# Four row norms of the retention ahead of the next units' states, one rotation behind two scores, first logits a half job later

## The chip, the cores and the metric

The kernel runs on one core of a Trainium2 chip. The metric is the device time of one execution in microseconds (us), the lower the better. Matrix products are done by TensorE (PE in the profile), most other arithmetic by VectorE (DVE), ScalarE (ACT) and GpSimd (POOL); SyncE (SP) issues most transfers. Each engine works through its own instructions in program order and waits on semaphores for the others.

## What is computed

One step of a one-layer streaming encoder on 512 prompt tokens, 64 sample tokens and 16 meta tokens, width 1024:

```
h = rmsnorm(x) @ w_in                        # rq, rk, rv, rg, sq, sk, sv
o_r = retention(rope(rq), rope(rk), rv)      # 4 heads, a state per head, chunk by chunk
o_r = rmsnorm(o_r) * silu(rg)                # per head: "row norm"
o_s = sliding_window_attention(sq, sk, sv)   # 8 query heads, 2 key heads, window 128
x = x + concat(o_r, o_s) @ w_out
x = x + moe(rmsnorm(x))                      # 32 experts, top group, then 2 in it
```

The experts' gate, up and down weights are 32 x 3 matrices of 1 MB; the router's logits come from the new x.

## The kernel before

The tokens are five tiles in the order `ORDER = [4, 0, 1, 2, 3]`; tile 4 (TAIL) holds the 64 sample and 16 meta tokens, the others 128 prompt tokens each. A *job* is the product of one tile with one 512-column chunk of w_in or w_out over half of the 1024 rows (12 matmuls, `job`, L1098; 8 for the tail, L1092). Jobs are numbered in the order of `halves()`: 10 for each of the chunks SKV, SQ, RQK, RV, RG and OUT0, OUT1 (the two halves of w_out). Weights are split into a high and a low part: ScalarE writes `w_hi` (L1648), GpSimd `w_lo` (L901).

All small work of retention, attention and router is hung between the jobs by `plan()`: for each job number s there are three lists, `before[s]`, `after[s]` and `behind[s]`, and the order of the whole program is before[s], job s, after[s], behind[s], for s = 0, 1, 2 and so on. **Every engine walks through this one list** and emits its own share of each step, so moving a step moves it on every engine that has a share in it. A step that only VectorE has a share in moves on VectorE alone.

The retention has ten units m = 0..9 (`RUNITS`: each tile twice, for the even and the odd heads). r0 is job 40, the first RG job. The steps of a unit:

- `ra` (two units at a time): TensorE the score products (L1230), VectorE the causal mask `ret_aT` (L2060).
- `ro` (two units at a time on TensorE): state increments (L1203), outputs of scores (L1257) and of the state (L1263). ScalarE squares the output (L1731). VectorE `ret_out`: two operations update the state (L2073, L2074, semaphore st_new), two form the mean square (L2076, L2079, semaphore ms_ready). GpSimd `ret_root`: eleven small operations (L316 to L326), then root_ready.
- `rn`, on VectorE alone (`ret_norm`): output times gate into `h_a` (L2107; waits for the gate), then times the root into `o_rows` (L2111; waits for root_ready).
- `rm`: TensorE transposes `o_rows` (L1291), VectorE multiplies by the gain (`part_r`, L2121), ScalarE writes the high part (L1737), VectorE the low part (L2126).

In the program order before, `rn` of units 1, 3 and 5 stands behind the `ro` of units (2, 3), (4, 5) and (6, 7), and `rn` of unit 6 behind the `ro` of (8, 9). The gate of a tile comes from its RG job (`gate_of`, L2090). `post(RQK, t)` is the rotary embedding of a tile's retention queries and keys (`rope`, L1911 to L1913, then L1971 and L1972), on VectorE; its first reader is the transpose `rT` (tile 0: job 39). The attention has 20 units; `score` (VectorE: row maxima, L2017 to L2025; ScalarE: exponentials), `norm` (VectorE, L2031 to L2034), `pT` (TensorE transposes of `probs`, L1170 and L1172), `value`.

After an OUT job VectorE adds it to x (`evict`, L2143). `square` is ScalarE's, `hT` transposes the new x on TensorE (L1302) and scales it on VectorE (L2155), `logit` multiplies by the router's weights on TensorE (L1313) and copies the result on VectorE (L2162, L2166). Behind the last logits come the choice of experts (VectorE), the gathering of rows and 16 pairs of experts (L1370 gate and up, L1385 down). SyncE loads their weights into a ring of 18 buffers of 1 MB; a load waits until TensorE has read what lay in its buffer:

```
sp.wait_ge(gu_ps, p - 2)
load_gu(p)
```

The first loads of experts' weights wait for all ten units' `rm`.

Of the kernel before, what the change touches and what calls it, by code (L numbers as in the profile page):

```python
# [21 lines left out]
TAIL = 4  # L22
# [32 lines left out]
SKV, SQ, RQK, RV, RG = range(5)  # L55
# [4 lines left out]
ORDER = [TAIL, 0, 1, 2, 3]  # L60
# [34 lines left out]
def plan():  # L95
# [3 lines left out]
    before = [[] for _ in range(len(lots) + 8)]  # L99
    after = [[] for _ in range(len(lots) + 8)]  # L100
    behind = [[] for _ in range(len(lots) + 8)]

    def done(c, t):
        return at[c, t, 1]
# [20 lines left out]
    for c in range(2, OUT0 + 2):  # L125
        first = at[c - 1, ORDER[0], 0]
        for k in range(KD):
            s = first + (k + 1 if k < 4 else 8 + (k - 4) // 2)
# [5 lines left out]
    s = done(SKV, ORDER[-1])  # L134
# [9 lines left out]
    for t in ORDER:  # L144
        s = done(SQ, t)
# [10 lines left out]
        before[s + 1 + n % 2].append(("norm", n))  # L156
        after[s + 3 + n % 2].append(("value", n))
    for t in ORDER:
        before[done(RQK, t) + 1].append(("post", RQK, t))
    before[30] += [("counts",)]  # L160
    for n, s in enumerate(starts):
        after[s + 2 + n % 2].append(("pT", n))
# [4 lines left out]
    r0 = at[RG, ORDER[0], 0]  # L167
# [4 lines left out]
        after[done(RG, t)].append(("gate", t))  # L172
    behind[done(RG, TAIL)].append(("gate2", TAIL))
    late = [3, 4, 5, 6, 7, 8, 11, 12, 13, 14]
    for m, (t, par) in enumerate(RUNITS):

        after[r0 + m // 2 * 2].append(("ra", m))
        (after if m > 1 else behind)[r0 + m // 2 * 2 + 1].append(("ro", m))
        before[r0 + late[m] - (1 if m > 5 else 0)].append(("rn", m))
    for m in reversed(range(len(RUNITS))):  # L180
        after[r0 + late[m]].insert(len(after[r0 + late[m]]) if m in (1, 3, 5, 6, 7) else 0, ("rm", m))
    after[r0 + len(RUNITS) + 1].append(("states_out",))
# [2 lines left out]
    for n in range(2):  # L185
        for i, t in enumerate(ORDER):
            s = done(OUT0 + n, t)
            after[s].append(("square", n, t))
            after[s + 1].append(("hT", n, t))
            after[s + 2].append(("logit", n, t))  # L190

    last = at[OUT1, ORDER[-1], 0]
    after[last - 1].append(("choose",))
# [136 lines left out]
def stream_step(nc, consts, x_prompt, x_sample, cache_ret_state, cache_swa_k, cache_swa_v,  # L330
# [21 lines left out]
    with ExitStack() as ctx:  # L352
# [334 lines left out]
        kv_out = sem("kv_out")  # L687

        STEPS = plan()

        def evicted(j):
# [1864 lines left out]
```

## Time and profile before

| | before |
|---|---|
| device time, median of 3 runs | 555.42 us (555.2 to 555.72) |
| the profiled execution: its own time, its span | 555.36 us, 553.5 us |
| PE, PE weight load busy | 483.5 us (87%), 304.8 us (55%) |
| DVE, ACT, POOL busy | 271.9 us (49%), 132.6 us (24%), 155.2 us (28%) |
| moved by DMA, mean | 144.74 MB, 262 GB/s |

The span runs from the first to the last instruction; the 1.86 us between it and the execution's own time lie around it. The shares are means over stages with different limits, so the rows below are read by stage. All row times are us from the start of the span. "[0.82 <-DVE o_rows L2111]" at the end of a row says how long the engine had stood idle just before, and which instruction ended that.

### The profile page before, as it was taken

Reading aid. Unit: us, or ns where it says so; the run is one execution under the profiler, and the core shown is the slowest. Engines: PE = TensorE matmul, PEld = TensorE weight load, DVE = VectorE, ACT = ScalarE, POOL = GpSimd, SP = SyncE. Lnnn points to the kernel's source line nnn. Section 1 sums busy time; section 2 is a strip of 40 time slices with the busy share of each in tenths; the row PEclk is TensorE's granted clock in tenths of the full one; section 3 lists DMA queues with packets and bytes.
Section 4 is the critical chain, followed back from the end, with each engine's and each line's share of the span. In section 5 each row is a group of like instructions: output and inputs, shape, how many; then the busy total and the mean of one; then the engine's idle time right before and its main releaser. Section 6 shows DMA issues by size and latency. Waiting matters only on the chain.

```text
span 553.5 us, 7556 instructions
## 1 busy us (share of the span) xinstructions
PE 483.5 (87%) x2748; PEld 304.8 (55%) x2748; DVE 271.9 (49%) x619; ACT 132.6 (24%) x361; POOL 155.2 (28%) x280
## 2 busy tenths in 40 slices
PE   4976989899999999899993999889999868878884
PEld 4955867677776677678883743233433323233232
DVE  2869679888455575742267422313332222022535
ACT  4754355465455223222111100000000000000010
POOL 5445773042024455823003300111112111000003
PEclk9989999899998999999996899979999999889998
DMA  8440220130039603249969699999999999999996
GB/s 299 161 126 7 76 77 2 35 119 1 2 124 319 234 8 102 83 178 401 388 249 422 234 342 420 408 420 417 424 416 418 419 423 418 418 422 420 414 399 216
DMA packets 35031, 144.74 MB, mean 262 GB/s; under 512 B 5842, under 2 KB 8994, under 8 KB 23216
## 3 DMA queue, kind: packets, MB, share of 16 engines
q1 hardware_dynamic: 26320, 129.94, 60.0%
q0 software_dynamic: 4528, 9.01, 4.5%
q10 hardware_dynamic: 4144, 5.28, 2.9%
q8 instruction: 23, 0.38, 0.3%
q14 instruction: 16, 0.13, 0.1%
HBM read 138.16 MB, written 17.30 MB: 281 GB/s over the span
## 4 chain that ended last, share of the span: by engine, by line
PE 44%; DVE 16%; DMA 14%; SPq 11%; issue 5%; ACT 5%; POOL 1%; DVEq 0%; ACTq 0%; POOLq 0%
PE banks L1098 15%; PE banks L1370 10%; SPq L743 7%; DMA w_moe_b<-in_w_up_dram 5%; PE banks L1385 4%; SPq L751 3%; DMA w_moe_b<-y_d 3%; DMA y_d<-rows,idx 2%; PE banks L1364 2%; DMA rows<-hn_d,idx 1%; DMA y_d<-y_sb,idx 1%; ACT w_hi L1648 1%; PE banks L1460 1%; PE banks L1313 1%; PE banks L1160 1%
## 5 line engine op out<-in xcount | busy, mean ns | idle before, releaser
L901 POOL TENSOR_TENSOR w_lo<-w_raw,w_hi 128x512 fp32r<-128x512 f32 x52 | 70.2, 1365 | 112.1 <-ACT w_hi L1648 110.6
L1370 PE MATMUL banks<-w_moe_b,xgT 128*64 128x512 f32 x224 | 66.9, 618 | 10.6 <-DMA w_moe_b<-in_w_up_dram 6.8
L1370 PE MATMUL banks<-w_moe_a,xgT 128*64 128x512 f32 x224 | 67.7, 626 | 4.2 <-DMA w_moe_a<-in_w_up_dram 4.2
L2376 DVE SCALAR_TENSOR_TENSOR glu_b<-banks,wr,glu_a 128x256 f32<-128x256 f32 x15 | 7.2, 483 | 96.5 <-ACT glu_a L1780 96.5
L1780 ACT ACTIVATE glu_a<-banks,wr 128x256 f32<-128x256 f32 x15 | 7.1, 473 | 196.2 <-PE banks L1370 183.3
L1098 PE MATMUL banks<-w_hi,xT_hi_a 128*128 128x512 f32 (+3 forms) x124 | 51.1, 412 | 1.5 <-DVE xT_lo_a L1842 1.5
L1098 PE MATMUL banks<-w_lo,xT_hi_a 128*128 128x512 f32 (+3 forms) x124 | 48.7, 393 | 0.0
L1098 PE MATMUL banks<-w_hi,xT_lo_a 128*128 128x512 f32 (+3 forms) x124 | 48.5, 391 | 0.0
L1370 PEld LDWEIGHTS banks<-w_moe_b,xgT 128*64 128x64 f32 x224 | 20.9, 142 | 49.4 <-issue 46.6
L1098 PE MATMUL banks<-w_hi,xT_hi_b 128*128 128x512 f32 (+3 forms) x92 | 35.6, 387 | 0.8 <-issue 0.8
L1370 PEld LDWEIGHTS banks<-w_moe_a,xgT 128*64 128x64 f32 x224 | 21.4, 144 | 26.0 <-issue 24.3
L1098 PE MATMUL banks<-w_lo,xT_hi_b 128*128 128x512 f32 (+3 forms) x92 | 34.1, 370 | 0.0
L1098 PE MATMUL banks<-w_hi,xT_lo_b 128*128 128x512 f32 (+3 forms) x92 | 33.9, 369 | 0.0
L1648 ACT CAST w_hi<-w_raw 128x512 fp32r<-128x512 f32 x52 | 30.8, 614 | 12.5 <-DMA w_raw<-in_w_out_dram 11.1
L1385 PE MATMUL banks<-w_moe_a,actT 128*64 128x512 f32 x144 | 32.6, 593 | 0.5 <-DVE actT L2393 0.5
L1098 PEld LDWEIGHTS banks<-w_hi,xT_hi_a 128*128 128x128 f32 (+1 forms) x124 | 24.2, 195 | 7.0 <-ACT xT_hi_b L1590 1.7
L1701 ACT ACTIVATE probs<-banks,soft,rstd_hq 128x208 f32<-128x208 f32 x36 | 18.6, 519 | 35.2 <-DVE soft L2025 35.2
L1098 PEld LDWEIGHTS banks<-w_hi,xT_lo_a 128*128 128x128 f32 (+1 forms) x124 | 24.1, 195 | 5.1
L1098 PEld LDWEIGHTS banks<-w_lo,xT_hi_a 128*128 128x128 f32 (+1 forms) x124 | 24.3, 196 | 3.9
L951 POOL DMA_INDIRECT rows<-hn_d,idx x7 | 7.2, 1032 | 58.4 <-DMA y_d<-rows,idx 47.6
L2339 DVE TENSOR_TENSOR xgT<-banks,g_both 128x1024 f32<-128x1024 f32 x15 | 18.3, 1217 | 10.6 <-PE banks L1364 10.6
L1385 PEld LDWEIGHTS banks<-w_moe_a,actT 128*64 128x64 f32 x144 | 11.0, 137 | 19.9 <-issue 19.2
(361 smaller groups left out, 910.1 us busy)
## 6 DMA issues: line engine op xcount, KB each, us to landing
w_moe_a<-in_w_down_dram SPq DMA_DIRECT2D x20, 1024.0 KB, 20.4
w_moe_a<-in_w_gate_dram SPq DMA_DIRECT2D x16, 1024.0 KB, 12.1
w_moe_a<-in_w_up_dram SPq DMA_DIRECT2D x16, 1024.0 KB, 14.3
w_moe_b<-in_w_gate_dram SPq DMA_DIRECT2D x14, 1024.0 KB, 17.0
w_moe_b<-in_w_up_dram SPq DMA_DIRECT2D x14, 1024.0 KB, 17.3
w_moe_b<-in_w_down_dram SPq DMA_DIRECT2D x10, 1024.0 KB, 25.8
w_raw<-in_w_in_dram SPq DMA_DIRECT2D x34, 256.0 KB, 4.1
y_d<-in_consts_dram SPq DMA_DIRECT2D x9, 512.0 KB, 10.0
```

Source lines behind the costliest of these rows:

```text
L743: sp.dma_start(units(gu_at(p, e, m), 1)[:, 0, :], v[2 * p + e]).then_inc(gu_in[p % 4], 16)
L751: sp.dma_start(dn_at(p, e), down_v[2 * p + e]).then_inc(dn_in[p % 4], 16)
L901: nc.gpsimd.tensor_tensor(w_lo[:, s, :], w_raw[:, s, :], w_hi[:, s, :].bitcast(F32), ALU.subtract).then_inc(split, 1)
L951: pool.indirect_dma_start(out=xg(p), out_offset=None, in_=hn_d, in_offset=bass.IndirectOffsetOnAxis(ap=idx[:, p:p + 1], axis=0), bounds_ch ...
L1098: l = mm(into[0:R, 0:width], a, w, start=(kk == 0 and q == 0), stop=(kk == KD - 1 and q == 2))
L1364: l = nc.tensor.transpose(into[:, k // 4, (k % 4) * P:(k % 4) * P + P], gv[:, k, :], ident)
L1370: l = mm(acc[64 * e:64 * e + 64, u, :].rearrange("p (m f) -> p m f", m=2), xgT[:, xu, k, 64 * e:64 * e + 64], units(at_e[e], 2)[:, :, k * ...
L1385: l = mm(acc[64 * e:64 * e + 64, 2 + n, :], actT[:, j, 64 * e:64 * e + 64], mats[e][:, j * D + n * 512:j * D + n * 512 + 512], start=(j == ...
L1648: nc.scalar.copy(w_hi[:, s, :], w_raw[:, s, :]).then_inc(hi_done, 1)
L1701: af(probs[:, q, c2, :], sideA[:, b, 256 * c2:256 * c2 + KEYS], ACT.Exp, scale=rstd_hq[:, t, c2, u:u + 1], bias=soft[:, q, 2 + c2:3 + c2], ...
L2339: tt(xgT[:, u], at[:, 0:2, :].rearrange("p b (j n) -> p (b j) n", j=4), g2T.unsqueeze(2).to_broadcast([P, KD, P]), ALU.mult).then_inc(xg_e ...
L2376: stt(out=glu_b[:, :], in0=acc[:, u, 0:FF], scalar=scales[0], in1=glu_a[:, :], op0=ALU.mult, op1=ALU.mult).then_inc(done, 1)
```

## The change

Three edits to `plan()`; no instruction is added, removed or changed in shape.

```diff
     for t in ORDER:
-        before[done(RQK, t) + 1].append(("post", RQK, t))
+        (behind if t == ORDER[1] else before)[done(RQK, t) + 1].append(("post", RQK, t))
...
     late = [3, 4, 5, 6, 7, 8, 11, 12, 13, 14]
+    sooner = {2: 1, 4: 3, 6: 5, 8: 6}
     for m, (t, par) in enumerate(RUNITS):
 
         after[r0 + m // 2 * 2].append(("ra", m))
+        if m in sooner:
+            after[r0 + m // 2 * 2 + 1].append(("rn", sooner[m]))
         (after if m > 1 else behind)[r0 + m // 2 * 2 + 1].append(("ro", m))
-        before[r0 + late[m] - (1 if m > 5 else 0)].append(("rn", m))
+        if m not in sooner.values():
+            before[r0 + late[m] - (1 if m > 5 else 0)].append(("rn", m))
...
-            after[s + 2].append(("logit", n, t))
+            after[s + (3 if n == 0 and t == TAIL else 2)].append(("logit", n, t))
```

What it does to the list of steps:

- `rn` of unit 1 goes from before job 44 to behind job 43, ahead of `ro` 2 and 3; `rn` 3 from before 46 to behind 45, ahead of `ro` 4 and 5; `rn` 5 from before 48 to behind 47, ahead of `ro` 6 and 7; `rn` 6 from before 50 to behind 49, ahead of `ro` 8 and 9. All of these lie behind the gate or `rm` step of the same job.
- `post(RQK, 0)` goes from before job 24 to behind it: on VectorE it then follows `value` 4 and `score` 6 and 7, and still precedes `norm` 6, which is the first step before job 25.
- `logit` of the first half of the tail goes from behind job 53 to behind job 54, after `rm` 9 and just ahead of `hT` of tile 0.

## Rows read from the trace of the kernel before

**Rows 1.** Windows: busy us (count) of PE, PEld, DVE, ACT, POOL; granted clock; DMA share; GB/s

```profile
183.00:290.00 107.00, 101.11 (x559) 79.67 (x559) 56.10 (x140) 24.40 (x57) 39.86 (x106) 1.00 0.54 203
294.70:308.10 13.40, 6.59 (x24) 5.76 (x24) 9.48 (x43) 1.76 (x4) 2.23 (x8) 0.50 0.87 362
...
329.00:520.00 191.00, 168.40 (x792) 66.93 (x791) 54.37 (x83) 7.24 (x15) 25.31 (x25) 0.96 1.01 415
```

**Rows 2.** Waits, 180 to 240 us: who waited for whom, us in total, times, longest

```profile
PE banks L1291 <- DVE o_rows L2111: 4.3, 4, 1.8
```

**Rows 3.** Timeline of TensorE: start, us, line, count, idle before

```profile
193.97 0.33 PE L1291 MATMUL banks<-cst,o_rows 64*128 64x64 f32 x2 [0.82 <-DVE o_rows L2111]
...
205.11 0.44 PE L1291 MATMUL banks<-cst,o_rows 128*128 128x128 f32 x2 [0.83 <-DVE o_rows L2111]
...
216.16 0.44 PE L1291 MATMUL banks<-cst,o_rows 128*128 128x128 f32 x2 [0.84 <-DVE o_rows L2111]
...
225.80 0.50 PE L1092 MATMUL banks<-w_hi,xT_hi_a 128*128 128x512 f32 x1 [0.30 <-POOL w_lo L901]
...
228.31 0.44 PE L1291 MATMUL banks<-cst,o_rows 128*128 128x128 f32 x2 [1.77 <-DVE o_rows L2111]
...
236.53 0.63 PE L1313 MATMUL banks<-w_router,xgT 128*64 128x36 f32 x8 [1.21 <-DVE xgT L2155]
```

**Rows 4.** Timeline of VectorE in the retention

```profile
190.04 0.42 DVE L2073 TENSOR_TENSOR h_b<-banks,state_p 64x256 f32<-64x256 f32 x1 [1.27 <-ACT squares L1731]
...
193.04 0.42 DVE L2107 TENSOR_TENSOR h_a<-banks,gate 64x256 f32<-64x256 f32 x1
193.49 0.42 DVE L2111 TENSOR_TENSOR o_rows<-h_a,root_r 64x256 f32<-64x256 f32 x1
...
198.44 1.53 DVE L2126 TENSOR_TENSOR xT_lo_a<-part_r,xT_hi_a 128x256 fp32r<-128x256 f32 x1 [0.47 <-ACT xT_hi_a L1737]
...
201.17 0.42 DVE L2073 TENSOR_TENSOR h_b<-banks,state_p 64x256 f32<-64x256 f32 x1 [0.55 <-ACT squares L1731]
...
212.22 0.42 DVE L2073 TENSOR_TENSOR h_b<-banks,state_p 64x256 f32<-64x256 f32 x1 [2.31 <-ACT squares L1731]
...
222.61 0.42 DVE L2073 TENSOR_TENSOR h_b<-banks,state_p 64x256 f32<-64x256 f32 x1 [1.72 <-ACT squares L1731]
```

**Rows 5.** Timeline of GpSimd: ends of roots, start of a pair of roots, the splits behind it

```profile
183.27 0.19 POOL L326 TENSOR_TENSOR root_r<-root_r 64x2 f32<-64x2 f32 x1
...
198.04 0.19 POOL L326 TENSOR_TENSOR root_r<-root_r 128x2 f32<-128x2 f32 x1
198.41 1.27 POOL L901 TENSOR_TENSOR w_lo<-w_raw,w_hi 128x512 fp32r<-128x512 f32 x1 [0.18 <-POOL root_r L326]
...
209.30 0.20 POOL L326 TENSOR_TENSOR root_r<-root_r 128x2 f32<-128x2 f32 x1
213.71 0.19 POOL L316 TENSOR_SCALAR root_r<-ms_r 128x2 int32<-128x2 int32 x1 [4.21 <-DVE ms_r L2079]
...
220.56 5.19 POOL L901 TENSOR_TENSOR w_lo<-w_raw,w_hi 128x512 fp32r<-128x512 f32 x4 [0.18 <-POOL root_r L326]
```

**Rows 6.** Timeline of ScalarE behind the last states

```profile
231.91 0.94 ACTq L1745 DMA_DIRECT2D out_dram<-state_p  x2
...
234.09 0.40 ACT L1737 CAST xT_hi_a<-part_r 128x256 fp32r<-128x256 f32 x1
```

**Rows 7.** Timeline of VectorE and TensorE around `norm` 6

```profile
101.01 0.59 DVE L2034 TENSOR_TENSOR probs<-probs,soft 128x416 f32<-128x416 f32 x1
...
101.66 0.44 PE L1170 MATMUL banks<-cst,probs 128*128 128x128 f32 x2 [2.25 <-DVE probs L2034]
```

**Rows 8.** The chain that ended last: two jobs of twelve matmuls

```profile
103.55 4.46 PE banks L1098 x12
...
109.09 2.79 PE banks L1098 x12
```

**Rows 9.** Timeline of SyncE's queue

```profile
329.13 0.33 SPq L743 DMA_DIRECT2D w_moe_a<-in_w_gate_dram  x1
```

## Prediction, made before the changed kernel was run

> **What bounds the kernel now.** I read the windows first [rows 1]. From 183 to 290 us TensorE is busy for 101.1 of 107 us at full clock while the DMA engines have a share of 0.54: the projections and the retention are bound by TensorE, so an idle microsecond of TensorE there is a microsecond of the kernel. From 329 to 520 the DMA share is 1.01 at 415 GB/s: the experts are bound by the stream of weights. What matters is whether a gain before 290 gets through that stream. The first load of the saturated stretch is issued at 329.13 [rows 9], and by the code it waits for `gu_ps`, a product of TensorE, since its buffer must first be read. All earlier loads wait in the same way for work that follows the projections. So the stream starts when TensorE lets it, has a fixed length, and ends earlier by what TensorE gains. I count the gain in full.
>
> Next, who holds TensorE up. The table of waits from 180 to 240 has 4.3 us in four waits of the transposes of `rm` for `o_rows` [rows 2]. The timeline places them: 0.82 at 193.97, 0.83 at 205.11, 0.84 at 216.16 and 1.77 at 228.31, before `rm` of units 1, 3, 5 and 6. Two more are small: 0.30 at 225.80 for a `w_lo` of GpSimd, 1.21 at 236.53 before the first logits [rows 3].
>
> **The four norms.** A norm is two operations of 0.42 us, 0.87 from 193.04 to 193.91 [rows 4]. In the case of unit 1, VectorE did the states of 2 and 3 from 190.04, then the norm, and TensorE began its transpose at 193.97, 0.06 after the norm ended. Moved ahead of the states, a norm is ready some 3 us earlier, and the stall is gone if nothing else is late. What must hold:
>
> - *VectorE has a gap in front of the states.* It stood idle for 1.27, 0.55, 2.31 and 1.72 us before the four first state operations, always for ScalarE's squares [rows 4]. A norm of 0.87 fits into three of the gaps and delays the states of 4 and 5 by 0.3 us. Those states are read by TensorE only with the next tile, about 10 us later, so 0.3 costs nothing. Without the gaps each norm would put 0.87 on the states and on the masks behind them.
> - *The root is there.* An early `rn` that waits for `root_ready` holds `ro` behind it on VectorE, and through ms_ready also GpSimd. The roots of units 1 and 3 ended at 183.46 and 198.23, before VectorE is at the moved norm (188.8 and about 199.1). That of 5 ended at 209.50 [rows 5]. VectorE gets to it when `rm` 4 is done: 209.9 in the old timetable, 208.25 once 0.82 + 0.83 are saved. The root itself moves only by 0.5 (its mean square follows the states of 4 and 5, now started at 200.7 instead of 201.17), to 209.0. The norm's second operation then waits 0.3 and ends at 209.5, still ahead of the squares, which move from 212.22 to 210.57. The root of 6 belongs to the pair begun at 213.71, both over before the split at 220.56; the moved norm starts at about 218.4. All four fit, the third by about 1 us.
> - *GpSimd's splits.* Here a part is lost. Behind the roots of 6 and 7 GpSimd has four splits, 5.19 us from 220.56, ending 225.75; TensorE already waited 0.30 for the last at 225.80 [rows 3, 5]. The start of this run hangs on the mean square of unit 6 at 213.71, which comes from TensorE's outputs of tile 2. They lie ahead of the third stall, so they move by 0.82 + 0.83 = 1.65, not by 2.49. The last split ends at 224.1; TensorE, 2.49 earlier, would want it at 223.0. It waits 1.1 instead of 0.3: the third stall's 0.84 goes into a longer wait for `w_lo`.
> - The fourth, 1.77, is saved in full: `rn` 6 ends near 219.3, and `rm` 6 is wanted at 224.9. What is late next is `rn` 7, still behind the states of 8 and 9: with these at 220.1 and 4.7 us long as before, it ends at 225.8, against 227.9 when `rm` 7 is wanted.
>
> **The first logits.** Before, `hT` of the tail was held up on VectorE behind the low part of `rm` 7, and that behind ScalarE: it issued the states' transfers up to 232.85, did its square, and wrote the high part of `rm` 7 at 234.09 [rows 6]. With TensorE 3.4 us ahead, the whole chain moves by 3.4, since ScalarE is released by VectorE's `part_r` of unit 6, which follows the `evict` of job 51; the transposed tail is ready at about 231.9. At its old place TensorE would want it at 231.75 and stall for 0.2 (1.3 if a GpSimd split holds VectorE there). At the new place, after job 54 and `rm` 9, it is wanted at 234.8: no stall. That takes 1.21. On VectorE the clear of the logits and the copy (0.4 us together) move behind `rm` 9 and ahead of the scaling of tile 0's transpose, wanted only a job later. The new neighbour to watch is `hT` of tile 0 on TensorE, which needs `evict` of job 53: ready at 234.5, wanted at 235.4. No transfer is moved past any queue by these edits; the early experts' loads start some 5 us sooner, with the end of `rm` 9, ahead of the second half of w_out's weights as before.
>
> **The rotation.** It goes behind `value` 4 and the scores 6 and 7, but stays ahead of `norm` 6. TensorE stood idle for 2.25 us before 101.66 for exactly this norm, which ran from 101.01 [rows 7]; VectorE has the same operations to do ahead of it in either order, so the norm ends when it did. ScalarE gets its exponentials 3 us sooner and VectorE saves a wait after the norm, but no TensorE wait follows there until the stage ends. Its reader, `rT`, is 15 jobs away. I take 0. The bounds: were the stall to vanish, 2.25, and with it the slow stretch behind it, where a job took 4.46 us against 2.79 at full clock [rows 8]: 3.9 together. If the order costs, then by one contended operation of about 1.1 us.
>
> **Sum.** 0.82 + 0.83 + 0.84 + 1.77 + 1.21 = 5.47, less 0.84 for the splits: 4.6. The profiled execution took 555.36, the median is 555.42, so 0.06 apart; 555.42 - 4.6 gives **550.8 us**. One term I can't place: TensorE ran at granted clock 0.50 from 294.7 to 308.1 [rows 1], after the logits. If the return to full clock does not move with the work, up to 1.7 us more or less of it are slow, which is up to 0.9 either way; I take 0.
>
> **The rivals.**
>
> - *VectorE gives much of it back by contention* (0.13). One `L2126` took 1.53 us instead of 0.42, started at 198.44 just behind a split of GpSimd at 198.41 and ending 0.3 after it [rows 4, 5]. The moved norms of 3 and 6 come right beside splits, at about 199.5 and 218.9 to 224.1, and the last writes of `rm` 7 and 8 may too. Two or three hits of 1.1 in a row between 218 and 234 add 2.2 to 3.3; 0.9 of it is slack before tile 0's `hT`. Gain 2.2 to 3.3, 552.1 to 553.2. The Trainium skill (SBUF — State Buffer, "Who interferes with whom") says that a VectorE operation with two SBUF inputs and a GpSimd operation reading SBUF exclude each other, so that the second blocks fully; by that rule this rival is what moving a norm beside a split does, and the trace of this case agrees with its 1.53 us.
> - *GpSimd's splits keep up* (0.08): the four splits finish sooner (fewer neighbours) and the 0.84 is kept, with the 0.30: 549.7 to 550.0.
> - *The rotation frees `norm` 6 after all* (0.05): 3.9 more, 546.9.
> - *No change* (0.06): the stream of weights takes up the gain, because a load before 329 hangs on bytes and not on TensorE. Against it: [rows 9]. 555.4.
> - *Slower* (0.03): the early norms wait for roots, with states, masks and GpSimd's next roots queued behind them. It decides the sign when a root comes later than the squares by more than the stall it removes, about 1.4 + 1.2 us after the time I gave for unit 5. With two chains of roots late (3.3 us each, 6.6 for the pair before 220.4) each of four norms costs up to 1.9 beyond its slack, 7.6 against 5.5 gained: 557.5. Against it are the times of the roots in [rows 5].
>
> **How the numbers follow.** My forecast, the sum with its GpSimd term, has 0.65: 550.8, of its own 549.7 to 551.9, by the clock term of 0.9 and 0.2 for rounding. The contended case adds 0.13 above it, the kept splits 0.08 below, the rest lies outside. The range 549.4 to 553.2 takes in these three less their edges, about 0.8. Within 0.2% (1.1 us) of 555.42 is what a measurement of this kernel can't tell from no change. Faster: 0.65 + 0.13 + 0.08 + 0.05 = 0.91; the same 0.06; slower 0.03.
>
> **What would show it.** In the profile after, the waits of L1291 for `o_rows` are gone or below 0.2 us in sum; the wait of L1092 for `w_lo` at about 224 has grown from 0.30 to about 1.1; the wait of L1313 at the first logits is gone; `rm` 9's transposes come about 5 us earlier than before, the first saturated load at about 324.5 instead of 329.13, and the 2.25 us before `norm` 6's transposes are unchanged. I am wrong if a new wait for `o_rows`, `ret_aT` or `x_sb` stands in the retention, if `root_ready` holds VectorE for over 1 us, or if TensorE's clock falls in a further stretch between 183 and 290 us: each job in it costs 1.7.

## The result, and the profile after

| | before | after |
|---|---|---|
| device time, median | 555.57 us (555.2 to 556.88) | 550.43 us (546.18 to 551.61) |
| ratio after to before, 95% interval | | 0.9859 (0.9823 to 0.9894) |
| the profiled execution: its own time, its span | 555.36 us, 553.5 us | 550.74 us, 548.9 us |

The kernel became faster. The comparison puts the gain at 7.8 us (5.9 to 9.8, by the ratio of 555.57), which is 547.6 us against 555.42: more than I forecast, and below the low end of my range, 549.4. The plain median of the four executions, 550.43, lies near the forecast; they reach from 546.18 to 551.61, wider than my whole allowance for the clock. So there are two questions: did the predicted waits go, and were they of the size I gave them?

Lines of the changed kernel stand 4 higher (L1291 is now L1295, L901 is L905). The table of waits of the kernel after, 175 to 240 us (who waited for whom: us in total, times, longest), answers to [rows 2]. TensorE's wait of the transposes for `o_rows` has no row any more. What is left for TensorE is `w_lo`:

```profile
PE banks L1096 <- POOL w_lo L905: 0.8, 2, 0.5
```

TensorE's timeline of the kernel after, against [rows 3]: start, duration, line, shapes, count, idle before.

```profile
193.18 0.72 PE L1234 MATMUL banks<-rT 64*128 64x128 f32 x8
193.73 0.28 PE L1295 MATMUL banks<-cst,o_rows 64*128 64x64 f32 x2
...
203.92 0.44 PE L1295 MATMUL banks<-cst,o_rows 128*128 128x128 f32 x2
...
214.06 0.44 PE L1295 MATMUL banks<-cst,o_rows 128*128 128x128 f32 x2
...
223.29 0.50 PE L1096 MATMUL banks<-w_hi,xT_hi_a 128*128 128x512 f32 x1 [0.34 <-POOL w_lo L905]
...
224.53 0.50 PE L1096 MATMUL banks<-w_hi,xT_hi_a 128*128 128x512 f32 x1 [0.50 <-POOL w_lo L905]
224.87 0.39 PE L1096 MATMUL banks<-w_lo,xT_hi_a 128*128 128x512 f32 x1
225.09 0.38 PE L1295 MATMUL banks<-cst,o_rows 128*128 128x128 f32 x2
...
234.68 0.38 PE L1295 MATMUL banks<-cst,o_rows 128*128 128x128 f32 x2
234.99 0.66 PE L1317 MATMUL banks<-w_router,xgT 128*64 128x36 f32 x8
```

All four stalls before `rm` of units 1, 3, 5 and 6 are gone, and so is the one before the first logits (the last row stands without a bracket). The wait for `w_lo` has grown from 0.30 to 0.84, in two pieces.

VectorE and GpSimd of the kernel after, against [rows 4, 5]; first VectorE:

```profile
190.79 0.42 DVE L2077 TENSOR_TENSOR h_b<-banks,state_p 64x256 f32<-64x256 f32 x1 [0.49 <-ACT squares L1735]
...
199.97 0.98 DVE L2115 TENSOR_TENSOR o_rows<-h_a,root_r 128x256 f32<-128x256 f32 x1
...
208.64 0.42 DVE L2111 TENSOR_TENSOR h_a<-banks,gate 128x256 f32<-128x256 f32 x1
...
209.49 0.43 DVE L2115 TENSOR_TENSOR o_rows<-h_a,root_r 128x256 f32<-128x256 f32 x1 [0.44 <-DVE h_a L2111]
...
211.02 0.42 DVE L2077 TENSOR_TENSOR h_b<-banks,state_p 64x256 f32<-64x256 f32 x1 [1.11 <-ACT squares L1735]
...
219.20 1.45 DVE L2115 TENSOR_TENSOR o_rows<-h_a,root_r 128x256 f32<-128x256 f32 x1
```

```profile
199.39 1.27 POOL L905 TENSOR_TENSOR w_lo<-w_raw,w_hi 128x512 fp32r<-128x512 f32 x1 [0.18 <-POOL root_r L330]
...
209.16 0.20 POOL L330 TENSOR_TENSOR root_r<-root_r 128x2 f32<-128x2 f32 x1
...
212.51 0.19 POOL L320 TENSOR_SCALAR root_r<-ms_r 128x2 int32<-128x2 int32 x1 [3.16 <-DVE ms_r L2083]
...
219.10 5.37 POOL L905 TENSOR_TENSOR w_lo<-w_raw,w_hi 128x512 fp32r<-128x512 f32 x4 [0.18 <-POOL root_r L330]
```

Times of two traces are compared best from a common point: `rm` 0 stands at 185.89 before and at 186.64 after, so what comes after it is another 0.75 us earlier, counted from there, than the printed times say. The norms sit in VectorE's gaps: before the states of 4 and 5, and of 8 and 9, no idle time is left, before those of 6 and 7 1.11 us. The root of unit 5 ended at 209.36, and `rn` 5 went on at 209.49, 0.44 late by the row (forecast 0.3); the row names `h_a`, which was done at 209.06, so it is the root that it waited for. GpSimd's four splits begin at 219.10, 1.46 earlier by the printed times and 2.21 earlier behind `rm` 0 (34.67 us before, 32.46 after; forecast 1.65). Two of the moved norms were caught beside a split and took 0.98 and 1.45 us in place of 0.42: the contention of the rival case came, and no wait of TensorE for a norm followed it. The Trainium skill (SBUF — State Buffer, "Who interferes with whom") has the second such operation blocked until the first is done, and the trace agrees: the norm at 199.97 started 0.58 us into its split and ended 0.29 us after that split's end at 200.66; the norm at 219.20 started 0.10 into the first of the four, which took 1.27, and ended 0.28 after it.

The last matters are the stream of weights and the clock. First SyncE's queue of the kernel after, against [rows 9], then its windows against [rows 1] (columns as there):

```profile
324.28 0.33 SPq L747 DMA_DIRECT2D w_moe_a<-in_w_gate_dram  x1
```

```profile
183.00:290.00 107.00, 104.52 (x594) 82.85 (x590) 58.07 (x146) 26.47 (x61) 46.01 (x124) 1.00 0.60 226
290.00:304.00 14.00, 7.19 (x24) 6.30 (x25) 10.26 (x44) 1.91 (x4) 3.08 (x7) 0.51 0.86 352
324.00:520.00 196.00, 175.36 (x812) 70.33 (x810) 56.24 (x85) 7.87 (x16) 25.32 (x25) 0.95 1.01 414
```

TensorE is busy for 104.5 of the same 107 us, against 101.1. The saturated stretch begins 4.85 us earlier (5.60 behind `rm` 0) and keeps its rate. From this load to the end both kernels take 224.4 to 224.6 us. So the gain does pass through the stream.

### The profile page after: what moved, and what is told of

It is laid out like the page before. It is cut to its first block, busy times and chain, and to the rows that moved or that the text cites. A ratio compares the mean times of both kernels' runs of the same rounds, so it can differ in the third digit from the quotient of the medians.

```text
span 548.9 us, 7556 instructions
## 1 busy us (share of the span) xinstructions
PE 486.0 (89%) x2748; PEld 307.0 (56%) x2748; DVE 271.1 (49%) x619; ACT 132.6 (24%) x361; POOL 156.1 (28%) x280
## 4 chain that ended last, share of the span: by engine, by line
PE 47%; DVE 14%; DMA 13%; SPq 11%; issue 4%; ACT 4%; POOL 2%; DVEq 0%; POOLq 0%; ACTq 0%
PE banks L1102 17%; PE banks L1374 10%; SPq L747 7%; DMA w_moe_b<-in_w_up_dram 5%; PE banks L1389 4%; SPq L755 3%; DMA w_moe_b<-y_d 3%; DMA y_d<-rows,idx 2%; PE banks L1368 2%; DMA rows<-hn_d,idx 2%; PE banks L1317 2%; DMA y_d<-y_sb,idx 1%; PE banks L1164 1%; PE banks L1464 1%; ACT w_hi L1652 1%
## 5 line engine op out<-in xcount | busy, mean ns | idle before, releaser
L905 POOL TENSOR_TENSOR w_lo<-w_raw,w_hi 128x512 fp32r<-128x512 f32 x52 | 71.0, 1382 | 108.6 <-ACT w_hi L1652 107.2
L1374 PE MATMUL banks<-w_moe_a,xgT 128*64 128x512 f32 x224 | 69.9, 647 | 4.5 <-DMA w_moe_a<-in_w_up_dram 4.5
L1389 PE MATMUL banks<-w_moe_a,actT 128*64 128x512 f32 x144 | 32.6, 593 | 0.5 <-DVE actT L2397 0.5
```

Of the source, the lines that this page charges most:

```text
L905: nc.gpsimd.tensor_tensor(w_lo[:, s, :], w_raw[:, s, :], w_hi[:, s, :].bitcast(F32), ALU.subtract).then_inc(split, 1)
L1374: l = mm(acc[64 * e:64 * e + 64, u, :].rearrange("p (m f) -> p m f", m=2), xgT[:, xu, k, 64 * e:64 * e + 64], units(at_e[e], 2)[:, :, k * ...
L1389: l = mm(acc[64 * e:64 * e + 64, 2 + n, :], actT[:, j, 64 * e:64 * e + 64], mats[e][:, j * D + n * 512:j * D + n * 512 + 512], start=(j == ...
```

## The yardstick for the experiments

Single executions of this program differ by far more than the stage in question, so I read every trace by six points on TensorE and SyncE: the first transposes of `rm` (unit 0), the last ones (unit 9), the last `hT` of a token tile, the product of the first pair of experts, the first saturated load, and the end. All in us. The column rm0-hT is the sum of the two ahead of it, and it is the one that the change works on. The last column lists the stretches in which TensorE's granted clock was about 0.50 (half of full clock, so 1.2 GHz), to the microsecond, from windows of each trace up to 325 us.

```
run    span   to rm 0  rm0-rm9  rm9-hT  rm0-hT  hT-pair  pair-load  load-end  clock 0.50 in
before 553.5  185.89   54.07    52.36   106.43  20.30    16.51      224.37    31-35, 103-107, 175-182, 294-308
f1     553.7  184.49   54.44    52.36   106.80  21.34    16.51      224.56    32-36, 175-180, 227-231, 292-309
f2     555.1  186.59   54.27    52.37   106.64  21.32    16.51      224.04    48-52, 102-110, 177-181, 228-233, 293-311
f3     557.3  185.72   54.08    52.43   106.51  23.15    17.84      224.08    31-35, 103-107, 174-182, 294-318
f4     554.9  185.60   54.42    52.31   106.73  21.38    16.51      224.68    33-37, 177-181, 228-232, 293-310
after  548.9  186.64   48.04    52.81   100.85  20.28    16.51      224.62    37-41, 102-110, 177-181, 290-304
e1     552.0  187.91   48.01    53.17   101.18  21.33    16.51      225.07    33-37, 105-109, 177-184, 289-307
e13    545.4  182.77   48.05    52.87   100.92  20.45    16.52      224.74    34-38, 47-52, 286-301
e2     552.8  188.69   49.53    52.32   101.85  21.42    16.52      224.32    34-38, 106-110, 177-185, 290-308
e3     551.6  181.73   54.38    52.42   106.80  21.30    16.51      225.26    33-37, 46-50, 224-228, 289-306
e4     554.8  186.72   52.05    53.29   105.34  21.75    16.51      224.48    34-38, 105-110, 177-181, 293-311
e5     550.5  187.00   48.23    52.85   101.08  21.31    16.51      224.60    32-36, 104-108, 176-183, 288-306
e7     554.8  188.02   51.02    53.16   104.18  21.58    16.51      224.51    37-41, 102-109, 177-184, 228-232, 293-311
e8     553.2  189.40   48.32    53.25   101.57  21.32    16.51      224.40    38-42, 103-111, 178-186, 291-309
e9     551.9  184.80   48.23    53.40   101.63  23.31    17.69      224.47    32-36, 110-118, 288-313
e10    551.6  187.90   47.41    52.85   100.26  21.76    16.51      225.17    33-37, 105-109, 177-184, 289-307
e12    552.0  188.39   47.39    52.95   100.34  21.69    16.51      225.07    34-38, 105-109, 177-185, 290-307
```

In the five traces of the kernel before (before, f1 to f4) the stage from `rm` 0 to the last `hT` takes 106.43 to 106.80 us, mean 106.62; in the three of the whole change (after, e1, e13) 100.85 to 101.18, mean 100.98. That is 5.6 us, with a scatter of 0.2. "to rm 0", hT-pair, pair-load and load-end scatter by up to 7.7, 3.0, 1.3 and 1.2 us, with no step between the kernels that stands out of that. The rotation lies ahead of `rm` 0 in either order, so the column rm0-hT doesn't test it.

## Experiments

**Which part does it?** The whole change again, and each edit alone.

`e1_all` is the change unchanged.

> The whole change, unchanged, in more executions. Theory A (the change is worth what its stage shows, 5.4 to 5.9 us between 183 and 295 us; the single executions of 546.2 to 551.6 differ by when TensorE's clock is halved in stages that the change does not touch): the executions spread again over 546 to 552 with a mean 5 to 6 us under that of the kernel before, and the trace has halved-clock stretches ahead of 183 us that differ from those of the first trace, with the same waits behind 183. Theory B (the change is worth some 8 us, since the rotation also removes clock loss around 100 us in most executions): a median near 547.5 and no halved stretch around 103.

Measured: 552.13 us (546.33 to 556.77), ratio 0.9869 (0.9812 to 0.9925), 7.3 us of 557.49, interval 4.2 to 10.5. The stage in its trace is 101.18. A stretch at half clock stands at 105 to 109, so the sign that theory B named isn't there.

`e2_norms_only`:

```diff
+    sooner = {2: 1, 4: 3, 6: 5, 8: 6}
...
+        if m in sooner:
+            after[r0 + m // 2 * 2 + 1].append(("rn", sooner[m]))
...
+        if m not in sooner.values():
```

> The four norms alone. Theory A: the waits for o_rows are gone (4.3 us), a wait for the logits of the tail stays, 0.2 to 1.3 us; 550.5 to 551.5, 4 to 5 us under before. Theory B: 551 or more, since the rotation's share is missing.

Measured: 552.99 us, ratio 0.9917 (0.9887 to 0.9948), 4.6 us (2.9 to 6.3). The stage takes 101.85, 4.8 less than before. A third wait before logits appears, of 0.45, for the first ones. The norms carry most of the gain.

`e3_rotation_only`:

```diff
-        before[done(RQK, t) + 1].append(("post", RQK, t))
+        (behind if t == ORDER[1] else before)[done(RQK, t) + 1].append(("post", RQK, t))
```

> The rotation alone. Theory A: the wait before the transposes of norm 6 stays at 2.1 to 2.3 us, norm 7 comes about 1 us sooner, the time is that of before within 0.5 us. Theory B: 2 to 4 us under before, with the halved stretch around 103 us missing in most executions.

Measured: 556.94 us, ratio 1.0004 (0.9966 to 1.0041). In the times the rotation can't be told from nothing, within some 2 us either way. Its stage is 106.80, but that lies behind the rotation. What its trace shows ahead of it is taken up at `e5_no_rotation`.

`e4_logit_only`:

```diff
-            after[s + 2].append(("logit", n, t))
+            after[s + (3 if n == 0 and t == TAIL else 2)].append(("logit", n, t))
```

> The tail's first logits a half job later, alone. Theory A: the 1.21 us wait of the logits goes, nothing else, so 1.0 to 1.3 us under before. Theory B says the same of this edit; a rival to both: VectorE is what is late here (hT of the tail behind rm 7), so the wait only moves to tile 0's hT or to rm 9, and the time is that of before.

Measured: 556.94 us, ratio 1.0009 (0.9986 to 1.0033). In the trace the wait before the first logits is gone and the stage is 105.34, 1.3 less than before. In its place stands 0.3 us, in the table of waits of e4, 180 to 250 us, for the x of tile 0, the neighbour that the forecast named:

```profile
PE banks L1302 <- DVE x_sb L2143: 0.3, 1, 0.3
```

So the trace has the expected 1.0 to 1.3 and the times don't: their interval reaches from a gain of 0.8 to a loss of 1.8 us. What was missing between the two is not settled; the other columns of the table vary by more than this. One part can be read from f1 below: in executions in which half clock follows unit 6's stall, the wait before the first logits isn't there in the kernel before either, and this edit has nothing to take away.

`e5_no_rotation` is the change with the rotation at its old place.

> The norms and the logits, with the rotation at its old place. Theory A (the rotation is worth nothing): from the first rm to the last hT of tokens the stage takes 100.9 to 101.2 us as in the whole change (106.4 before), the time is that of the whole change, 5 to 6 us under before. Theory B (the rotation is worth some 1.5 us in the whole change, as the difference of the runs of the whole change and of the norms alone would have it): 4 to 4.5 us under before.

Measured: 552.15 us, ratio 0.9886 (0.9854 to 0.9917), beside 0.9859 and 0.9869 for the whole change. The stage of 101.08 fits theory A, but it begins behind the rotation and so doesn't decide. The way past `norm` 6 does. From the transposes of `norm` 5 to those of `norm` 6 TensorE takes 10.80 or 10.81 us in all eight traces with the rotation at its old place, and 10.68 or 10.69 in all eight with it moved (e9 is another order): 0.12 saved. Then the clock matters. In two traces of either order no half clock follows `norm` 6. Here is TensorE's next wait in f1 (old place), and in e13 (moved):

```profile
112.20 0.34 PE L1194 MATMUL banks<-probsT,v_own 80*64 80x64 f32 x4 [1.56 <-ACT probsT L1713]
```

```profile
112.04 0.34 PE L1198 MATMUL banks<-probsT,v_own 80*64 80x64 f32 x4 [0.34 <-ACT probsT L1717]
```

f4 has the same 1.56, e3 the same 0.34. From the transposes of `norm` 6 to TensorE's wait for `probsT` at about 134 us it takes 32.19 in f1 and f4, 30.97 and 30.99 in e13 and e3. Where about 3.5 us of half clock follow `norm` 6, as in the recorded trace of before, the wait of 1.56 isn't there, and it takes 32.47 to 32.54 in the old order and 32.49 to 32.51 in the new one. So the rotation is worth 1.3 us in an execution with full clock there, and 0.1 in one with such a stretch. Over the eight traces of either order the means don't differ in its favour (32.6 and 32.7), since the new order has more of the stretches of some 7 us (three against one). No net gain is shown, but it isn't nothing in each execution.

**Does the rotation gain little because it stays ahead of `norm` 6?** `e9_rotation_behind_norm` puts it behind that norm:

```diff
-        (behind if t == ORDER[1] else before)[done(RQK, t) + 1].append(("post", RQK, t))
+        (behind[done(RQK, t) + 2] if t == ORDER[1] else before[done(RQK, t) + 1]).append(("post", RQK, t))
```

> The whole change, but the rotation of tile 0 also behind norm 6 (after value 5, ahead of norm 7). Theory A: the wait of TensorE before the transposes of norm 6, 2.1 us, is gone or below 0.3, and the stretch of halved clock behind it (3.4 or 6.8 us in four of five traces, half of that lost) goes in most executions: 2.3 to 5 us under the whole change. Rival: VectorE is only late with the next, norm 7 or the scores 8 and 9, and TensorE waits there instead: no gain.

Measured: 552.61 us (548.85 to 553.66), ratio 0.9882 (0.9849 to 0.9914), beside 0.9886 for e5. Rows of e9, first VectorE's `norm` 6, then ScalarE and TensorE behind it:

```profile
98.32 0.59 DVE L2038 TENSOR_TENSOR probs<-probs,soft 128x416 f32<-128x416 f32 x1
...
107.69 0.58 DVE L2024 TENSOR_REDUCE soft<-banks 128x2 f32<-128x416 f32 x1
```

```profile
109.03 0.52 ACT L1705 ACTIVATE probs<-banks,soft,rstd_hq 128x208 f32<-128x208 f32 x1 [8.11 <-DVE soft L2029]
```

```profile
112.20 0.48 PE L1198 MATMUL banks<-probsT,v_own 80*64 80x64 f32 x4 [3.91 <-ACT probsT L1717]
```

The norm starts at 98.32, and TensorE's wait for `probs` falls to 0.2 us in the whole stretch. But now the rotation holds up the row maxima of the next scores, ScalarE idles for 8.11 us, and TensorE waits 3.91 for its `probsT`. The wait has moved and grown, from 2.14 (after) to 3.91. My rival on the stall of [rows 7], that the freed norm is worth up to 3.9 us, gets no support even when the norm is really freed. What the norm alone would be worth, without the new wait, isn't measured.

**How large is each stall, and what does GpSimd take back?** `e8_norm5_left` leaves the third norm at its old place:

```diff
-    sooner = {2: 1, 4: 3, 6: 5, 8: 6}
+    sooner = {2: 1, 4: 3, 8: 6}
```

> The whole change but for the norm of unit 5, which stays behind the states of 6 and 7. Theory A (GpSimd's four splits stand behind the roots of 6 and 7 and take up a part of the third stall): a wait of 0.8 for o_rows of unit 5 is back, the wait for w_lo falls from 0.84 to about 0.3, so the stage gets longer by only 0.4 to 0.6 us. Rival (the wait for w_lo has another cause, such as a later write of w_hi): w_lo stays at 0.8 and the stage is 1.0 us longer.

Measured: 554.97 us in one execution. TensorE's timeline of e8:

```profile
217.73 0.44 PE L1295 MATMUL banks<-cst,o_rows 128*128 128x128 f32 x2 [0.83 <-DVE o_rows L2115]
...
227.59 0.50 PE L1096 MATMUL banks<-w_hi,xT_hi_a 128*128 128x512 f32 x1 [0.49 <-POOL w_lo L905]
```

The stall of 0.83 is back and the wait for `w_lo` falls from 0.84 to 0.49. From `rm` 0 to `rm` 9 it takes 48.32 against 48.03 us: by the distances between the `rm`, unit 5's comes 0.91 later and then 0.60 of it is made up before unit 6's, so only 0.3 shows there (0.6 by the last `hT`, for a wait in w_out's second half that comes and goes, below). So the term for GpSimd in the sum is real: TensorE, early, waits for splits that are not early.

`e7_norm6_left` leaves the fourth:

```diff
-    sooner = {2: 1, 4: 3, 6: 5, 8: 6}
+    sooner = {2: 1, 4: 3, 6: 5}
```

> The whole change but for the norm of unit 6. Theory A (the idle time that the profile prints before a transposing matmul is short by 0.1 to 0.2 us of what the stall costs, since the end of the matmul ahead is modelled): the profile prints about 1.8 us of wait for o_rows again, and the stage from the first rm to the last hT is longer by 1.9 to 2.1. Rival (printed waits are exact, and the surplus over the forecast has other causes): longer by 1.7 to 1.8 at most. With the w_lo wait in front of it as in the whole change (0.84).

Measured: 556.56 us in one execution; TensorE's timeline of e7:

```profile
224.76 0.50 PE L1096 MATMUL banks<-w_hi,xT_hi_a 128*128 128x512 f32 x1 [0.43 <-POOL w_lo L905]
...
226.00 0.50 PE L1096 MATMUL banks<-w_hi,xT_hi_a 128*128 128x512 f32 x1 [0.50 <-POOL w_lo L905]
...
227.85 0.44 PE L1295 MATMUL banks<-cst,o_rows 128*128 128x128 f32 x2 [1.13 <-DVE o_rows L2115]
```

The printed idle time is 1.13, not the 1.8 expected, and the stage is 104.18, longer by 3.2 than with the norm moved, not by 2. Behind the stall the clock stood at half from 228 to 232. The distances between the `rm` part the 3.2: `rm` 6 comes 1.38 later behind `rm` 5 (12.41 against 11.03), `rm` 7 another 1.61 behind `rm` 6 (4.61 against 3.00), which is the half clock, and 0.2 comes after `rm` 9. On the size of a stall theory A holds: from the last matmul ahead of `rm` 6 at 226.34 to 227.85 are 1.51 us, 0.22 in the kernel after, so the stall cost 1.29 where 1.13 is printed. That it is 1.13 and not 1.77 has a plain reason: TensorE had waited 0.93 for `w_lo` just before, in place of 0.30, and what it waits there it doesn't wait again. So with norm 6 left, the longer wait for `w_lo` costs only 0.3 (12.41 from `rm` 5 to `rm` 6, against 12.15 in the kernel before).

`e10_splits_ahead` takes two of the four `w_lo` splits out of the run behind the roots and puts them ahead of the roots of 6 and 7, on top of the whole change:

```diff
-            after[s] += weights(ENTRY[c, k])
+            after[s] += [x for x in weights(ENTRY[c, k]) if x[0] == "hi" or c != OUT0 or k not in (4, 5)]
...
+        if m == 6:
+            after[r0 + 7] += [("lo", ENTRY[OUT0, 4]), ("lo", ENTRY[OUT0, 5])]
```

> The whole change, with the first two of the four splits of GpSimd ahead of the roots of units 6 and 7. Theory A: GpSimd uses its idle time before these roots, the wait of TensorE for w_lo (0.84) goes, the stage is 0.8 to 1.0 us shorter, 99.9 to 100.3 us from the first rm to the last hT. Rival: the root of 6 comes 1.3 to 2.6 us later, its early norm waits for it with the states of 8 and 9 behind it, and a wait for o_rows of unit 7 appears: no gain or a loss.

Measured: 553.37 us in one execution; GpSimd of e10, then TensorE:

```profile
213.04 2.52 POOL L907 TENSOR_TENSOR w_lo<-w_raw,w_hi 128x512 fp32r<-128x512 f32 x2 [2.43 <-ACT w_hi L1654]
...
222.45 2.65 POOL L907 TENSOR_TENSOR w_lo<-w_raw,w_hi 128x512 fp32r<-128x512 f32 x2 [0.18 <-POOL root_r L332]
```

```profile
225.16 0.50 PE L1098 MATMUL banks<-w_hi,xT_hi_a 128*128 128x512 f32 x1 [0.48 <-POOL w_lo L907]
```

Two splits go first, two are left behind the roots, which start 2.1 us later behind `rm` 0 than in the change; of the 0.84 a wait of 0.48 remains. The stage takes 100.26, 0.7 less than the 100.98 of the change. The same kernel was then timed, beside the change itself:

> The whole change with two splits ahead of the roots of 6 and 7, now timed, as the version that could beat both. Theory A: its stage is 0.5 to 0.7 us shorter, so a time of 0.987 of before less 0.001, which these rounds can't tell from the whole change. Rival (the single profiled execution was the odd one): the stage is again 100.9 to 101.2 us.

> The whole change, unchanged, on the same chip as the other runs of this call. Theory A: ratio to before 0.987 to 0.991 (5 to 7 us), single executions from 546 to 557, and the stage at 100.9 to 101.2 us. Theory B (the change is worth 7.3 to 7.9 us, as the two ratios so far say): ratio at or below 0.987 again.

Measured: `e12_splits_timed` 551.25 us (546.34 to 553.78), ratio 0.9866 (0.9827 to 0.9905), stage 100.34; `e13_all_again` 549.01 us (547.3 to 556.4), ratio 0.9858 (0.9819 to 0.9897). No wait for `o_rows` of unit 7 came, so the rival falls. The 0.6 to 0.7 us that the stage shows twice can't be told in the times.

**Does a stall cost clock as well?** In e7 the clock fell behind unit 6's stall, and in the recorded execution of before it hadn't. If it did so in most executions of before, the change would gain more than the recorded one tells: an explanation for 7.8 in place of 5.6. Four more traces of the kernel before, unchanged:

> The kernel before, unchanged, one more look. Theory C (the stalls that the change takes away, above all the 1.77 us at unit 6, also bring a stretch of halved clock behind them in a part of the executions, as the traces with that stall and the rotation alone, and with norm 6 left, showed it at 224 to 232 us): of four looks one to three have a halved stretch between 215 and 245 us, and their stage from the first rm to the last hT is 107 to 109 us against 106.4 without. Theory A (what exceeds the stalls is only the scatter of the unchanged stages): no such stretch in four looks, all stages at 106.4.

> The kernel before again, same expectations as for the first of these looks.

> The kernel before again, same expectations as for the first of these looks.

> The kernel before again, same expectations as for the first of these looks.

Measured: 555.45, 557.0, 559.04 and 556.81 us. TensorE's timeline of f1:

```profile
226.93 0.64 PE L1291 MATMUL banks<-cst,o_rows 128*128 128x128 f32 x2 [1.79 <-DVE o_rows L2111]
...
235.47 0.66 PE L1313 MATMUL banks<-w_router,xgT 128*64 128x36 f32 x8
```

and a window of f1:

```profile
227.00:231.00 4.00, 4.00 (x12) 3.25 (x13) 3.40 (x8) 0.40 (x1) 2.81 (x13) 0.57 0.06 16
```

After the stall TensorE runs at half clock, 12 instructions in 4 us. That stretch stands in the 224 to 233 region of f1, f2, f4 and e3, but not of before, f3 and e4: in 4 of 7 traces with the norm of unit 6 at its old place and the other three norms too, and in e7. In none of the nine traces with that norm moved (after, e1, e2, e5, e8, e9, e10, e12, e13) is it there. So the stretch comes with the stall of unit 6, in about half of the executions, and the change ends that. But in the kernel before it costs little: f1, f2 and f4 have 106.64 to 106.80 for the stage, before and f3 106.43 and 106.51. The time that the slow clock takes is taken from the wait of 1.21 before the first logits, which in f1 stands without a bracket: there `rm` 7 comes 1.59 us late and `rm` 9 makes up 1.25 of it. In e7, where the logits are moved and no such wait follows, the same stretch costs the whole 1.61. I had expected 0.6 to 2.6 us of it; it is 0.1 to 0.4. The occurrence is shown, the cost refutes the explanation.

## Why the prediction was right, and where it was wrong

**Right.** The mechanism is the one predicted, at each place: the stalls of units 1, 3, 5 and 6 and the one before the logits are gone, and no new wait for `o_rows`, `ret_aT` or `x_sb` came. The splits of GpSimd take back what was forecast (table below; e8, e10). `rm` 9 comes 5.3 us earlier (forecast about 5) and the saturated stream begins at 324.28 (forecast about 324.5). That these two meet the forecast so well is luck: the kernel after reached `rm` 0 0.75 us later, in a stage that the norms don't touch, and behind `rm` 0 they come 6.0 and 5.6 us earlier. The stream's length stays within 224.0 to 225.3 us in all traces, so the rival "no change" falls. The rival of contention falls in a more useful way: the hits came and found slack, or nearly so. In e2, e5 and e9 GpSimd's splits start 32.74 us behind `rm` 0 instead of 32.46, and `rm` 6 comes 0.22 later; why these three differ wasn't tested.

**Wrong, first: the Sum.** The step that failed is the price of its terms. It gives 4.6 us where the stage, over five traces of before and three of the change, gives 5.6. I read each stall as the idle time printed before the matmul. A better price is the distance between the starts of TensorE's last instruction ahead of the stall and the first behind it, before and after. Here are the rows of TensorE in the kernel before that precede the first and the fifth row of [rows 3], and two of w_out's second half:

```profile
192.43 0.72 PE L1230 MATMUL banks<-rT 64*128 64x128 f32 x8
...
226.14 0.40 PE L1092 MATMUL banks<-w_lo,xT_hi_a 128*128 128x512 f32 x1
...
261.42 0.39 PE L1092 MATMUL banks<-w_lo,xT_hi_a 128*128 128x512 f32 x1
...
261.90 0.50 PE L1092 MATMUL banks<-w_hi,xT_hi_a 128*128 128x512 f32 x1
```

From 192.43 to 193.97 are 1.54 us; in the kernel after, from 193.18 to 193.73, 0.55. The stall cost 0.99, not 0.82. Unit 6 in the same way: from 226.14 to 228.31 are 2.17, and after, from 224.87 to 225.09, 0.22, so 1.95, not 1.77. For `w_lo`: from `rm` 5 to the last matmul that waits for it, 9.64 us before (216.16 to 225.80) and 10.47 after (214.06 to 224.53), so 0.83 more. The ends of matmuls are modelled, so an instruction that is printed as still running may already be done. The terms of the sum, read this way relative to the first `rm` of each recorded execution, against my numbers:

| term | forecast | measured |
|---|---|---|
| unit 1 | 0.82 | 0.99 |
| unit 3 | 0.83 | 0.95 |
| unit 5 | 0.84 | 0.91 |
| unit 6 | 1.77 | 1.95 |
| taken back by the wait for `w_lo` | -0.84 | -0.83 |
| first logits | 1.21 | 1.30 |
| behind them, to the last `hT` | 0 | 0.31 |
| sum | 4.63 | 5.58 |

The table reads down TensorE's timeline, so a small difference outside a stall is in the row that follows it. GpSimd took back what I forecast: the last split ends 2.03 us earlier behind `rm` 0 and TensorE wants it 2.85 earlier; I had 1.65 and 2.49, both too small, with nearly the same difference. The growth of the printed waits, 0.54, is again too small a price. The 0.31 is mostly a wait that no row prints: at 261.42 a matmul starts, and the next 0.48 later, where such neighbours stand 0.23 apart; GpSimd's last split of that half had ended at 261.85. The kernel after doesn't have it, nor has e13, but e1, the same program, has it (0.48 again). So this last term belongs to the recorded pair of executions, and not for certain to the change.

**Wrong, second: the rotation at 0.** I wrote that no wait of TensorE follows `norm` 6 until the stage ends. In f1 and f4 a wait of 1.56 us follows, and with the rotation moved it is 0.34. The recorded execution of before had half clock there, which hid it.

**Wrong, third: "How the numbers follow".** I allowed 0.9 us for the clock and 0.2 for rounding, from three executions that lay within 0.5 us. The 56 executions of the kernel before that stand beside the experiments reach from 552.87 to 563.23, the 16 of the whole change from 546.18 to 556.77. The traces show what differs: in stages that the norms and the logits don't touch, stretches at half clock come, last and go from one execution to the next. The way to `rm` 0 takes 181.7 to 189.4 us, the part from the last `hT` to the first pair 20.3 to 23.3. Three executions that agree are no measure of that, and the one stretch that I priced, behind the logits, lasts 13.6 us in before and after, 17.0 to 17.1 in f1, f4 and e1, and 23.9 in f3; for the 1.7 us from which the 0.9 came the prediction names no row, and no run shows it. With a gain of 5.6 in place of 4.6 and an honest spread, the range would have had to reach below the 547.6 that was measured.

**What stays open.** The ratios of the three timings of the whole change have their centres at 7.3 to 7.9 us, the stage at 5.6. The lower ends of the gains, 5.9, 4.2 and 5.7, lie around 5.6, so scatter is nearly enough; the differences of the plain means over all executions are smaller too, 6.1, 6.1 and 7.0, and so is that of the traces' spans, 6.1. The clock behind unit 6 adds only 0.1 to 0.4 and is already in the 5.6. The rotation can add up to 1.3 us in some executions; in how many was not measured. No run here separates the rest.

## What to carry to other kernels

A step whose inputs are ready early, on an engine that has a gap ahead of its next release, can be moved into that gap at no cost; look then for what else hangs on the stage that was late (here GpSimd's splits), because the bound engine will wait for that next. Price a stall by the distance between the starts on both sides of it, compared with the same place where nothing stalls, not by the idle time printed before it. Look whether a wait is missing from a trace only because half clock covers it there. And take the spread of single executions from several traces of the kernel before, stage by stage, ahead of giving a range.

## What the runs showed of the hardware that I had not expected

The same program gets different clocks. In the kernel before, the stall of about 2.2 us ahead of `norm` 6 is followed by half clock for 3.5 us (before, f3), for 6.8 us (f2) and not at all (f1, f4). In the whole change it is 6.9 us (after), 3.4 us (e1) and none (e13). Windows of e13, of the kernel after behind that stall, and of f3 behind the logits:

```profile
60.00:285.00 225.00, 216.80 (x1444) 167.72 (x1442) 143.50 (x373) 90.14 (x271) 88.53 (x198) 1.00 0.43 153
```

```profile
102.40:109.20 6.80, 6.80 (x29) 5.59 (x29) 6.38 (x17) 1.71 (x7) 0.00 (x0) 0.50 0.00 0
```

```profile
294.00:319.00 25.00, 18.16 (x81) 15.48 (x82) 13.76 (x52) 1.91 (x4) 6.62 (x13) 0.52 0.81 304
```

e13 has full clock for 225 us on end, with the same program and nearly the same stall as the kernel after, and its span is 3.5 us shorter. In f3 the last stretch takes 23.9 us (294.2 to 318.1) instead of 13.6, and its first pair of experts comes 2.9 us later. A halved stretch behind a wait costs only what isn't covered by the next wait, which is why the one at 227 in f1 cost 0.4 us at most, and the one at 228 in e7, with no wait behind it, 1.6.
